# Two narrow layer norms whose consumers take centred inputs, with the deviation applied when results are evicted

## The reference

```python
def layer_norm(x, g, b):
    xf = x.astype(jnp.float32)
    mu = jnp.mean(xf, axis=-1, keepdims=True)
    var = jnp.mean(jnp.square(xf - mu), axis=-1, keepdims=True)
    return ((xf - mu) * lax.rsqrt(var + LN_EPS)).astype(x.dtype) * g + b

def ffn_sublayer(h, shift, scale, gate, w_in, w_out, g, b):
    y = swiglu(modulate(h, shift, scale), w_in, w_out)
    return layer_norm(ALPHA * h + FFN_RES * gate * y, g, b)
...
        h_lat = layer_norm(ALPHA * h_lat + m_lat[5] * y_lat, ln_g[i, 1], ln_b[i, 1])
        h_lat = ffn_sublayer(h_lat, m_lat[6], m_lat[7], m_lat[8], ffn_w_in[i, 1], ffn_w_out[i, 1], ln_g[i, 2], ln_b[i, 2])
...
        x = x + 0.5 * _swiglu(_rms_norm(x, ffn1_norm[l]), ffn1_wi[l], ffn1_wo[l])
```

## Time and profile before

| | us |
|---|---|
| median of 3 runs | 2641.03 |
| the profiled execution | 2639.72 |
| its span (first to last instruction) | 2638.0 |
| PE busy | 2588.3 (98%) |
| DVE busy | 1663.0 (63%) |
| ACT busy | 1093.3 (41%) |
| POOL busy | 434.3 (16%) |

### The profile page before, as it was taken

One profiled execution on the slowest core, in us unless ns is written; L12 is line 12 of the kernel. 1 busy time (PEld: TensorE's weight loads), 2 busy tenths in 40 slices (PEclk: granted clock), 3 DMA queues, 4 the chain that ended last, 5 costly groups with the idle time before them and its releaser, 6 DMA issues.

```text
span 2638.0 us, 43300 instructions
## 1 busy us (share of the span) xinstructions
PE 2588.3 (98%) x17036; PEld 2295.6 (87%) x17036; DVE 1663.0 (63%) x2506; ACT 1093.3 (41%) x1559; POOL 434.3 (16%) x483
## 2 busy tenths in 40 slices
PE   8999999999999999999999989999999999999999
PEld 6888888867888888888889779989999999998999
DVE  6766747465674474675665765567676666666565
ACT  3222224265422223321224664454555555556453
POOL 4000024123400004300014130020101201100210
PEclk9999999999999999999999999999999999999999
DMA  7554524411253352454452125545433554532554
GB/s 294 172 179 160 189 97 149 153 51 64 97 190 130 110 182 89 137 201 146 145 173 94 57 97 199 177 167 200 149 113 128 191 194 166 194 128 87 186 183 161
DMA packets 64761, 394.40 MB, mean 150 GB/s; under 512 B 7552, under 2 KB 9056, under 8 KB 29664
## 3 DMA queue, kind: packets, MB, share of 16 engines
q1 hardware_dynamic: 43872, 317.17, 34.1%
q0 software_dynamic: 20192, 73.21, 8.3%
q10 hardware_dynamic: 544, 1.89, 0.2%
HBM read 391.19 MB, written 1.05 MB: 149 GB/s over the span
## 4 chain that ended last, share of the span: by engine, by line
PE 87%; DVE 6%; ACT 3%; issue 2%; POOL 1%; DMA 1%; SPq 0%; DVEq 0%; ACTq 0%; POOLq 0%
PE banks L456 23%; PE banks L457 23%; PE banks L458 23%; DVE wlo L381 2%; ACT whi L373 2%; PE banks L476 1%; PE banks L478 1%; PE banks L477 1%; PE banks L573 1%; PE banks L575 1%; PE banks L574 1%; PE banks L1635 1%; PE banks L1659 1%; PE banks L1646 1%; DMA scale_start<-in_w_mod_scale 1%
## 5 line engine op out<-in xcount | busy, mean ns | idle before, releaser
L381 DVE TENSOR_TENSOR wlo<-raw,whi 128x2048 fp32r<-128x2048 f32 (+1 forms) x262 | 640.2, 2444 | 347.8 <-ACT whi L373 347.8
L373 ACT CAST whi<-raw 128x2048 fp32r<-128x2048 f32 (+1 forms) x262 | 530.1, 2023 | 441.7 <-PE banks L458 398.0
L456 PE MATMUL banks<-uhi,whi 128*128 128x512 f32 (+1 forms) x1520 | 551.4, 363 | 3.1 <-DVE sums L1931 1.5
L457 PE MATMUL banks<-ulo,whi 128*128 128x512 f32 (+1 forms) x1520 | 550.3, 362 | 0.0
L458 PE MATMUL banks<-uhi,wlo 128*128 128x512 f32 (+1 forms) x1520 | 550.3, 362 | 0.0
L456 PE MATMUL banks<-u2hi,whi 128*128 128x256 f32 x1248 | 353.5, 283 | 0.9 <-DVE wlo L381 0.7
L458 PE MATMUL banks<-u2hi,wlo 128*128 128x256 f32 x1248 | 350.2, 281 | 0.0
L457 PE MATMUL banks<-u2lo,whi 128*128 128x256 f32 x1248 | 349.9, 280 | 0.0
L618 DVE SCALAR_TENSOR_TENSOR squares<-mod_slot,crow 128x1024 f32<-128x1024 f32 x256 | 313.2, 1224 | 31.1 <-DMA mod_slot<-in_w_mod 7.8
L456 PEld LDWEIGHTS banks<-uhi,whi 128*128 128x128 f32 x1520 | 285.1, 188 | 54.3 <-issue 1.8
L458 PEld LDWEIGHTS banks<-uhi,wlo 128*128 128x128 f32 x1520 | 285.1, 188 | 49.9
(11 more groups left out here) (458 smaller groups left out, 4872.4 us busy)
## 6 DMA issues: line engine op xcount, KB each, us to landing
raw<-in_ffn_in SPq DMA_DIRECT2D x132, 1024.0 KB, 4.9
raw<-in_ffn_out SPq DMA_DIRECT2D x48, 1408.0 KB, 6.2
mod_slot<-in_w_mod POOLq DMA_DIRECT2D x128, 512.0 KB, 3.8
raw<-in_w_merge SPq DMA_DIRECT2D x32, 1024.0 KB, 4.8
raw<-in_w_in SPq DMA_DIRECT2D x26, 1024.0 KB, 4.9
raw<-in_na_qkv SPq DMA_DIRECT2D x12, 1024.0 KB, 4.8
raw<-in_w_out SPq DMA_DIRECT2D x8, 1024.0 KB, 4.8
raw<-in_wa_qkv SPq DMA_DIRECT2D x6, 1024.0 KB, 4.8
```

The lines of the kernel that those rows point to most:

```text
L373: act.copy(whi[u % 2][:, 0:unit_size[u]], raw[u % 2][:, 0:unit_size[u]]).then_inc(hi_done, 1)
L381: dve.tensor_tensor(wlo[u % 2][:, 0:n], raw[u % 2][:, 0:n], whi[u % 2][:, 0:n].bitcast(F32), ALU.subtract).then_inc(lo_done, 1)
L456: pe.matmul(out, w_hi, x_hi[:, k, 0:T], start=(n == 0), stop=False)
L457: pe.matmul(out, w_hi, x_lo[:, k, 0:T], start=False, stop=False)
```

## The change

For s = 5 and 6 the inputs are centred and scaled by the feature's factor, but not divided by the deviation. The shift stands in two more columns of uhi and ulo, so those products have 258 columns, the last two of them the weights times the shift.

- PE (centred_first_unit): the mean is made first; the mean of squares comes behind the second chunk of the first unit. POOL adds h in pairs of chunks, and chunk 6 ahead of the squares of chunk 5.
- ACT copies the mean to SBUF, squares it, makes the eight high parts, then the second half split, then Ln and Exp. DVE subtracts the mean and makes the low parts in turn, then the variance, then its second half split.
- L1.ffn1.in0 and in1 are evicted by folded_in_act and folded_in_dve: both banks times rstd, a copy of the two shift columns (128x2) per unit, Silu with the shift as bias, and the up value with its shift added in the product. POOL multiplies h by rstd before the residual.
- M0.ffn0.in0: three units (CENTRED_UNITS) take inputs centred by norm 6. Their results times norm 6's rstd are kept in SBUF (early_evict_dve) until norm 7's rstd is there. Norm 6's h, the inputs u2hi and u2lo and the squares are made beside them; h is now made on ACT. The fourth unit is the first_unit, with the square means behind its chunks.

The core of the diff:

```diff
+    CENTRED_UNITS = 3
+
+    def centred_first_unit(pe, ph, s):
 
         u = ph.u0
+        mean_pe(pe, s, S, last_evicted(BEFORE_CENTRED[s]))
+        start_unit(pe, u)
+        for k in range(KC):
+            pe.wait_ge(*DVE_.at("centred input", s, k))
+            for half in range(2):
+                out = banks[:, bank(u, half), 0:S + 2]
+                w_hi, w_lo = (cols(t, u, k, half * P, half * P + P) for t in (whi, wlo))
+                pe.matmul(out, w_hi, uhi[:, k, 0:S + 2], start=(k == 0), stop=False)
+                pe.matmul(out, w_hi, ulo[:, k, 0:S + 2], start=False, stop=False)
+                mm = pe.matmul(out, w_lo, uhi[:, k, 0:S + 2], start=False, stop=(k == KC - 1))
+                if k == KC - 1:
+                    mm.then_inc(product, 1)
+            if k == 1:
+                means_pe(pe, s, S)
+
...
+            if mean and cc % 2 == 0 and cc < KC - 2:
+                sum_pool(pool, s, T, source, cc)
+                sum_pool(pool, s, T, source, cc + 1)
+            if mean and cc == KC - 3:
+                sum_pool(pool, s, T, source, KC - 2)
...
+    CENTRED_IN = {"L1.ffn1.in0": 5, "M0.ffn0.in0": 6}
+    centred_mean = sums[:, 1, S:T2]
...
+    def rstd_of(s, T):
+        return rstd[:, S:T2] if s == 6 else rstd[:, 0:T]
...
+    def early_result(j, half):
+        return (scaled, full_u)[half][:, j % 2, (j // 2) * S:(j // 2 + 1) * S]
+
+    def early_shift(j):
+        return small[:, 2 * j:2 * j + 2]
...
+        shift = centred_vectors(s)[1]
+        for i in range(2):
+            dve.tensor_copy(uhi[:, :, S + i], shift).then_inc(*DVE_.up())
+        dve.wait_ge(*DVE_.here())
+        for i in range(2):
+            dve.tensor_tensor(ulo[:, :, S + i], shift, uhi[:, :, S + i].bitcast(F32), ALU.subtract)\
+                .then_inc(*DVE_.up(("centred columns", s)))
...
+    def centred_hi_act(act, s, cc):
+        act.wait_ge(*DVE_.at("centred", s, cc))
+        act.activation(uhi[:, cc, 0:S], h[:, cc, 0:S], ACT.Identity, scale=centred_vectors(s)[0][:, cc:cc + 1])\
+            .then_inc(*ACT_.up(("centred hi", s, cc)))
+
+    def centred_lo_dve(dve, s, cc):
+        dve.wait_ge(*ACT_.at("centred hi", s, cc))
+        dve.scalar_tensor_tensor(ulo[:, cc, 0:S], h[:, cc, 0:S], centred_vectors(s)[0][:, cc:cc + 1],
+                                 uhi[:, cc, 0:S].bitcast(F32), ALU.mult, ALU.subtract)\
+            .then_inc(*DVE_.up(("centred input", s, cc)))
+
+    def early_evict_dve(dve, s, j):
+
+        u = CENTRED[s].u0 + j
+        b = bank(u, 0)
+        dve.wait_ge(product, 2 * u + 2)
+        dve.tensor_copy(early_shift(j), banks[:, b:b + 2, S]).then_inc(*DVE_.up())
+        for half in range(2):
+            ins = dve.tensor_tensor(early_result(j, half), banks[:, b + half, 0:S], rstd_of(s, S), ALU.mult)
+            if half:
+                ins.then_inc(evicted, 1)
+            else:
+                ins.then_inc(*DVE_.up(("early result", s, j)))
 
...
             act.wait_ge(*PE_.at("mean", s))
+            act.copy(centred_mean, banks[:, 4, 0:T]).then_inc(*ACT_.up(("mean copy", s)))
             act.activation(var[:, 0:T], banks[:, 4, 0:T], ACT.Square).then_inc(*ACT_.up(("mean2", s)))
+            act.wait_ge(*DVE_.at("centred columns", s))
+            for cc in range(KC):
+                centred_hi_act(act, s, cc)
             split_hi_piece(act, CENTRED[s].u0 + 1, 1)
             act.wait_ge(*DVE_.at("var", s))
...
+    CENTRED_AHEAD = 2
 
     def centre_dve(dve, s, T):
+        u = CENTRED[s].u0 + 1
+        split_lo_piece(dve, u, 0)
+        dve.wait_ge(*ACT_.at("mean copy", s))
+        for cc in range(CENTRED_AHEAD):
+            centre_chunk(dve, s, T, cc)
+        for cc in range(KC):
+            centred_lo_dve(dve, s, cc)
+            if cc + CENTRED_AHEAD < KC:
+                centre_chunk(dve, s, T, cc + CENTRED_AHEAD)
         dve.wait_ge(*ACT_.at("mean2", s))
         dve.wait_ge(*PE_.at("means", s))
         dve.tensor_tensor(var[:, 0:T], banks[:, 5, 0:T], var[:, 0:T], ALU.subtract).then_inc(*DVE_.up())
         dve.wait_ge(*DVE_.here())
         dve.tensor_scalar(var[:, 0:T], var[:, 0:T], 0.0, None, ALU.max).then_inc(*DVE_.up(("var", s)))
-        for cc in range(CENTRED_EARLY):
-            centre_chunk(dve, s, T, cc)
+        split_lo_piece(dve, u, 1)
...
+            if s == 5:
+                pool.wait_ge(*ACT_.at("rstd", s))
+                pool.wait_ge(*DVE_.at("centred input", s, cc))
+                pool.tensor_tensor(h[:, cc, 0:T], h[:, cc, 0:T], rstd_of(s, T), ALU.mult).then_inc(*POOL_.up())
+                pool.wait_ge(*POOL_.here())
+            else:
+                pool.wait_ge(*ACT_.at("full", s, cc))
...
     def last_norm1_dve(dve, s):
 
...
+        u0 = CENTRED[s].u0
+
+        def scale_chunk(cc):
+            dve.wait_ge(*DVE_.at("centred", s, cc))
+            dve.tensor_tensor(h[:, cc, 0:S], h[:, cc, 0:S], rstd_of(s, S), ALU.mult)\
+                .then_inc(*DVE_.up(("n", s, cc)))
+
         centre_dve(dve, s, S)
         dve.wait_ge(*ACT_.at("rstd", s))
...
+        early_evict_dve(dve, s, 0)
+        scale_chunk(0)
+        scale_chunk(1)
+        split_lo(dve, u0 + 2)
+        for cc in range(KC):
+            if cc == 3:
+                early_evict_dve(dve, s, 1)
+                split_lo(dve, u0 + 3)
+            if cc + 2 < KC:
+                scale_chunk(cc + 2)
+            dve.wait_ge(*ACT_.at("h", s, cc))
+            folded_lo_dve(dve, s + 1, cc)
+        early_evict_dve(dve, s, 2)
+        split_lo(dve, u0 + 4)
 
...
         rstd_act(act, s, S, True)
-        act.wait_ge(*DVE_.at("vX", s))
+        split_hi(act, u0 + 2)
         for cc in range(KC):
             act.wait_ge(*DVE_.at("n", s, cc))
             act.activation(u2hi[:, cc, 0:S], h[:, cc, 0:S], ACT.Identity, scale=vX1[:, cc:cc + 1],
                            bias=vX0[:, cc:cc + 1]).then_inc(*ACT_.up(("u hi", s + 1, cc)))
+            act.wait_ge(*ACT_.here())
+            act.activation(h[:, cc, 0:S], h[:, cc, 0:S], ACT.Identity, scale=vS1[:, s, cc, 0:1],
+                           bias=vS0[:, s, cc, 0:1]).then_inc(*ACT_.up(("h", s, cc)))
+            if cc == 2:
+                split_hi(act, u0 + 3)
             if cc >= SQUARES_BEHIND:
-                squares_act(act, s + 1, S, lambda k: DVE_.at("h", s, k), (cc - SQUARES_BEHIND,))
-        squares_act(act, s + 1, S, lambda k: DVE_.at("h", s, k), range(KC - SQUARES_BEHIND, KC))
-        split_hi(act, TAKES[s + 1].u0 + 2)
+                squares_act(act, s + 1, S, lambda k: ACT_.at("h", s, k), (cc - SQUARES_BEHIND,))
+        split_hi(act, u0 + 4)
+        squares_act(act, s + 1, S, lambda k: ACT_.at("h", s, k), range(KC - SQUARES_BEHIND, KC))
...
+            early = s == 7 and it is None and u < ph.u0 + CENTRED_UNITS
             if u == ph.u0 and s != 7:
-                split_hi(act, u + 2)
+                split_hi(act, u + (1 if name == "L1.ffn1.in1" else 2))
             act.wait_ge(f_scaled, plus(g + 1, 2, it))
-            act.activation(buf["a"][:, u % 2, 0:S], buf["a"][:, u % 2, 0:S], ACT.Silu).then_inc(f_silu, 1)
-            if it is not None or ph.u0 < u < ph.u0 + ph.n - 1:
+            if name in SHIFTED:
+                act.wait_ge(f_shift, plus(g + 1, 2, it))
+            shift = dict(bias=small[:, 2 * (u % 2):2 * (u % 2) + 1]) if name in SHIFTED else {}
+            act.activation(buf["a"][:, u % 2, 0:S], buf["a"][:, u % 2, 0:S], ACT.Silu, **shift).then_inc(f_silu, 1)
+            if not early and (it is not None or ph.u0 < u < ph.u0 + ph.n - 1 or name == "L1.ffn1.in1" and u == ph.u0):
                 split_hi(act, u + 2, it)
             act.wait_ge(f_full, plus(g + 1, 2, it))
             act.copy(buf["hi"][:, i, 0:S], buf["full"][:, u % 2, 0:S]).then_inc(f_hi, 1)
-        sweep(act, ph, one, 2)
+        sweep(act, ph, one, 2, CENTRED_UNITS if s == 7 else 2)
...
+            if s == 7 and it is None and u < ph.u0 + CENTRED_UNITS:
+                j = u - ph.u0
+                if f >= 2:
+                    dve.wait_ge(f_split, f - 1)
+                dve.wait_ge(*DVE_.at("early result", s - 1, j))
+                dve.wait_ge(evicted, u + 1)
+                dve.scalar_tensor_tensor(buf["a"][:, u % 2, 0:S], early_result(j, 0), early_shift(j)[:, 0:1],
+                                         rstd[:, 0:S], ALU.add, ALU.mult).then_inc(f_scaled, 1)
+                dve.scalar_tensor_tensor(buf["full"][:, u % 2, 0:S], early_result(j, 1), early_shift(j)[:, 1:2],
+                                         rstd[:, 0:S], ALU.add, ALU.mult).then_inc(*DVE_.up(("early up", s, j)))
+                dve.wait_ge(*DVE_.at("early up", s, j))
+                dve.wait_ge(f_silu, f + 1)
+                dve.tensor_tensor(buf["full"][:, u % 2, 0:S], buf["a"][:, u % 2, 0:S], buf["full"][:, u % 2, 0:S],
+                                  ALU.mult).then_inc(f_full, 1)
+                dve.wait_ge(f_hi, f + 1)
+                dve.tensor_tensor(buf["lo"][:, i, 0:S], buf["full"][:, u % 2, 0:S],
```

(27 more changed lines are left out.)

158 lines of the change are left out of this document (63 added, 95 removed).

## The result

| | before | after |
|---|---|---|
| median, 8 runs each on the same chip | 2640.52 | 2649.68 |
| lowest to highest | 2638.49 to 2643.12 | 2646.70 to 2652.86 |
| ratio after / before, 95% interval | | 1.0032 [1.0024, 1.0041] |
| profiled execution | 2639.72 | 2650.17 |
| its span | 2638.0 | 2648.5 |

By the ratio the kernel became slower by 8.5 us (6 to 11); the medians are 9.2 apart. 2648.0 was forecast, in a range of 2642.3 to 2652.3. A ratio is not the quotient of the two medians beside it; where the text gives a gain or a loss of a kernel, it goes by the ratio. First the waits of TensorE (PE) after the change, from L1.wo to the end of M0.ffn0.in0: line, what released it, us in total, times, longest.

A forecast was written before the change was run, and what follows sets the result against it. TensorE, busy 98% of the span, was taken as the bound. Norm 5's -2.9, +7.8, +2.0 and 0.1 for 144 wider matmuls gave +7.0: profiled 2646.7, median 2648.0 us, range 2642.3 to 2652.3.

The forecast's parts named there:

- The stall: M0.ffn0, between units 4 and 5: TensorE waits for unit 5's split behind the three held units; +7.8 us.
- the restart: M0.ffn0, unit 5: the 7.6 us pause drops TensorE's clock to half behind it; +2.0 us.
- The starts: Behind both norms: L1.ffn1's unit 1 begins 4.5 us earlier, M0.ffn0's unit 0 2.65 us earlier.
- The width: L1.ffn1: 258 columns cost 0.91 ns more than 256, on a line to 512, over 1008 matmuls; +0.9 us.
- steps over 5.7 in L1.ffn1: L1.ffn1: unit steps of 5.64 us were forecast; steps over 5.7 would show the forecast wrong.
- Rival 3: L1.ffn1 and M0.ffn0: wider matmuls cost more than the line, up to +140 us if like 512 columns; chance 0.02.
- The passages: L1.ffn1, two passages from in to out: hidden value later by copy and Silu, 0.35 us each; +0.7 us.
- Norm 5 in all: Norm 5 and L1.ffn1: earlier start less width and passages; -2.9 us.
- The clock in norm 5: Norm 5: unit 0 starts at half clock despite a short pause; by the skill's rule, 2.0 us more gain.
- Rival 1: Norm 7's round starts early, before M0.ffn0's unit 5, so not slower: sum -0.2 us, 2640.8; chance 0.17.
- Rival 2: M0.ffn0: no stall, as the change orders things otherwise than read; 2636 to 2638 us; chance 0.05.
- Rival 4: L1.ffn1 becomes bound by DVE and ACT, whose work is hidden by only 0.1 us; 2651.5 us; chance 0.06.

The follow-up runs named there:

- e2: The change at norm 6 only, with norm 5 as in the kernel before but POOL's new order kept; 1.0029 of the kernel before.
- e10: The change plus 56 matmuls with unused results between units 4 and 5 of M0.ffn0; 1.0030 of the kernel before.
- e4: The change with cast and split of M0.ffn0's unit 5 moved ahead of the kept units' processing on ACT and DVE; 1.0030 of the kernel before.
- e1: The change at norm 5 only, with norm 6 as in the kernel before but POOL's new order kept; 1.0000 of the kernel before.
- e3: Kernel before with unused extra columns in L1.ffn1 from in0's second unit: 264 in in0, 266 in in1; 0.1222 and 0.1233 us a matmul, run once.
- e7: Kernel before with unused extra columns in L1.ffn1 from in0's second unit: 320 in in0, 322 in in1; 0.1466 and 0.1489 us a matmul, run once.
- e6: The change at norm 5 only, without the shift: 256 columns, no copy of two columns, Silu without bias; 0.9988 of the kernel before.
- e11: Kernel before with additional matmuls keeping TensorE busy in the gaps of norms 5 and 6; 0.9989 of the kernel before.
- e5: Kernel before with centred inputs for only the first three units of L1.ffn1.in0, normalised inputs and 256 columns afterwards; 1.0003 of the kernel before.
- e9: As e5, with ACT and DVE reordered, Silu's table loaded ahead and matmuls filling both norms' gaps; 0.9993 of the kernel before.
- e12: As e9, with four centred units and each unit's cast, split and eviction ahead of the normalised chunks; 0.9984 of the kernel before.

## Why the prediction was right, and where it was not

The sign of the whole was right, and for norm 6 the place, the mechanism and the size. Norm 5 was forecast to gain 2.9 us and gains nothing in the runs; the term that failed there is the width.

- **The stall (+7.8) and the restart (+2.0).** Measured 7.5 and 2.1 in the trace; e2 shows them with norm 5 out of the way, e10 the restart by itself (1.7, the rest of the 2.1 being the slower rate), e4 that the order of ACT's queue is what the split waited for. The last square mean was forecast 34.6 us behind the end of L1.ffn1, and ends about 34.9 behind it. Unit 5 starts 14.8 us behind PE's last row of square means; 14.3 was forecast from its end, which is about a microsecond later. From the end of L1.ffn1 to unit 5 that makes 48.9 us forecast and 48.55 measured; the two errors cancelled in part.
- **The starts (-4.5 at unit 1 of norm 5, 2.65 at unit 0 of norm 6).** Measured -4.74 and 2.71. The first agreement is in part luck. In e1, e4 and e10, which have the change's norm 5, unit 1 starts 14.13, 14.09 and 13.91 us behind L1.wo's last matmul, not 12.78, as the clock stayed low for about 7 us and not 3.5. And in e3 and e7, which have the norm 5 of before, it starts at 17.03 and 17.23, not 17.52. So these profiles put the gain between 2.9 and 4.7.
- **The width (+0.9) failed.** "I take the line, as 258 lies next to 256": the line gives 0.9 ns a matmul, measured 3.3. Over 1056 matmuls of L1.ffn1 that is 3.5 us. The forecast's own sign ("steps over 5.7 in L1.ffn1", which are 5.76) is the one that came out wrong. The prediction worked out a line between two widths where no row had a width near 256; e6, without the two columns and their copy, keeps the start, and e3 finds the surcharge in the kernel before too. Rival 3, to which I gave little, was true in a small form: it did not need a matmul as slow as 512, only 2.4 ns more.
- **The passages (+0.7)** measured 0.9, their mechanism as told: PE's wait for the split went from 0.22 to 0.67.
- **Norm 5 in all (-2.9)** came out at 0 (e1, from -2.1 to +2.4), and so the sum of +7.0 was low; the traces have +9.6, the runs 8.5. Of the parts, the width cost 2.4 more than forecast (1008 matmuls at 2.4 ns) and the passages 0.2, and 0.7 went in out0 and out1, which the forecast did not touch.
- **The clock in norm 5.** It did fall again behind a pause as short as 3.0 us (0.78 in 1559 to 1560), as the forecast took from the earlier trace rows against the rule of the Trainium skill that it cites. But the reading of the earlier trace rows was too sure. "Had worked since" left out a second wait, of 0.54 us ahead of the squares' mean; and in e3 and e7, the same code up to there, the clock stayed at 1.00 until 1564.25 and 1564.5, inside the long wait, as that rule would have it. So one and the same code can go either way. The clock came back at 1563.0 in the change's profile, 2.9 us behind unit 0's start where 4.0 was forecast; in e1's it was low until 1566.0, 5.8 behind it. What I had not seen is that in the kernel before the half clock cost nothing within unit 0, since DVE's second half split paced unit 1 (e11); the forecast compared starts of unit 1 and so was not harmed by it.
- **Rival 1 (not slower)** needed the last square mean 31.4 us behind the end of L1.ffn1 (1785.3); it ended 34.9 behind it, 3.5 later than that and a little later than forecast. **Rival 2** (no stall) is out by the trace. **Rival 4** (L1.ffn1 bound by DVE and ACT) too: no wait in the middle of in0 or in1.

What stays open: the timing law of fp32r matmuls above 256 columns, the 0.1178 us below, what decides when the clock falls and how long it stays low, and whether norm 6 can be centred at a profit at all. With the cast moved (e4) and the clock held (e10) together it would by the traces still lose some 5 us (an estimate, 9.6 less 2.9 and 1.7 to 2.0); that was not run, nor were fewer centred units at norm 6.

## What to carry to other kernels

An early start behind a norm is paid once, but the columns, copies and scalings that make it possible are paid in every unit that uses them. Confine them to the units that run until the proper input is ready. Where results are kept back, list what stands behind their processing in each engine's fixed order: here a cast that could have run 11 us earlier stood behind four Silus. And a price read between two distant widths is not a price for two columns: measure the very shape; one profile is enough for it. A gain read between two single profiles is in doubt by as much as these differ in a stretch that the change leaves alone.

## What the hardware showed that was not expected

- Two columns more on a 256-column fp32r matmul cost 3.3 ns, 264 columns 5.5, 266 6.6 (table above).
- Matmuls of 256 columns that nothing holds back take 0.1167 us in some stretches and about 0.1178 in others, at a clock of 1.00, in the same code. Why stays open. The same window of in1, in the kernel before and in e5, which executes the same shapes there:

```profile
1670.00:1700.00 30.00, 30.00 (x260) 30.00 (x259) 16.80 (x17) 13.09 (x16) 0.00 (x0) 1.00 0.50 175
```

```profile
1670.00:1700.00 30.00, 30.00 (x257) 30.00 (x256) 16.05 (x17) 12.99 (x15) 0.00 (x0) 1.00 0.53 178
```

  In e5 it began with a passage and lasted at least to 1750. It is 1% of the stretch, about 1 us over out0 to out1, and part of why single profiles of one kernel differ.
- The time at half clock behind a pause differs between profiles for what looks like the same pause: in norm 5 from 1559.5 to 1563.0 in the change, 1559.0 to 1566.0 in e1, 1559.75 to 1570.0 before.
- When the clock falls differs too, and that moves the start of unit 0. Norm 5 in the kernel before, and in e3, which has the same code up to unit 1 (PE's timeline, and a window of each):

```profile
1560.47 1.06 PE L830 MATMUL banks<-squares,k 128*128 128x256 f32 x2
...
1560.00:1561.00 1.00, 1.00 (x4) 0.67 (x2) 0.00 (x0) 0.41 (x1) 0.00 (x0) 0.50 0.00 0
```

```profile
1560.56 0.59 PE L830 MATMUL banks<-squares,k 128*128 128x256 f32 x2
...
1560.00:1561.00 1.00, 0.98 (x4) 0.68 (x4) 0.00 (x0) 0.84 (x1) 0.00 (x0) 1.00 0.01 0
...
1564.00:1565.00 1.00, 0.00 (x0) 0.00 (x0) 0.84 (x4) 1.00 (x3) 0.09 (x1) 0.69 0.00 0
```

  In e3 the squares' mean still runs at full clock, the variance follows sooner, and unit 0 starts 8.71 us behind L1.wo's last matmul (8.77 in e7), 9.58 in the kernel before: 0.8 to 0.9 us without any change of code. Against e3 and e7 the change starts unit 0 3.9 us earlier, not 4.8. A gain of 2 us around such a place needs the median of many runs, or a look at the clock of each profile. What does hold the clock is work in the gaps: it is 1.00 in all of e9, e11 and e12 through both norms, and in e10 at the stall.
